# A two-layer diffusion backbone with 64 experts: the experts' down weights move from SyncE's DMA queue to ScalarE's

## What is computed

```python
scores = jax.nn.sigmoid(t @ router_w)              # 64 experts, groups of 8, the best 8 of 4 groups
gate = jnp.einsum('tk,tke->te', wts, jax.nn.one_hot(top_e, N_EXPERTS))
act = jax.nn.silu(jnp.einsum('td,edf->tef', t, w_gate)) * jnp.einsum('td,edf->tef', t, w_up)
routed = jnp.einsum('tef,efd->td', act * gate[:, :, None], w_down)
shared = (jax.nn.silu(t @ sh_gate) * (t @ sh_up)) @ sh_down
```

## Time and profile before

| | us |
|---|---|
| median of 3 runs | 1647.92 (1643.26 to 1652.52) |
| the profiled execution, its own time | 1641.82 |
| its span in the trace | 1640.2 |
| TensorE busy | 1474.5 |
| ScalarE busy | 260.6 |
| VectorE busy | 460.2 |

### The profile page before, as it was taken

The page is one execution under the profiler, slowest core; times in us unless marked ns, Lnnn a source line. Parts: engine busy times, 40 slices in busy tenths (PEclk is TensorE's granted clock), DMA queues, the critical chain, the costliest instruction groups (busy, mean ns, idle before and its releaser), DMA issues. The chain is left out here.

```text
span 1640.2 us, 28207 instructions
## 1 busy us (share of the span) xinstructions
PE 1474.5 (90%) x12120; PEld 781.4 (48%) x12121; DVE 460.2 (28%) x956; ACT 260.6 (16%) x441; POOL 107.2 (7%) x349
## 2 busy tenths in 40 slices
PE   3899988999898989899869998989999999999995
PEld 3665755634343434344346667564344334334441
DVE  1291875311110111111134548470111111111112
ACT  1223103311010111111013221051111111111110
POOL 2600520000000000000000024000000000000000
PEclk8899999899999999999979999989999999999998
DMA  6755940499999999899744778008999999999994
GB/s 244 254 186 209 327 168 1 192 388 408 387 421 388 418 387 418 361 422 405 329 172 148 273 255 305 7 38 350 407 380 418 375 413 381 418 389 385 395 422 181
DMA packets 109253, 509.56 MB, mean 311 GB/s; under 512 B 12865, under 2 KB 14653, under 8 KB 59197
## 3 DMA queue, kind: packets, MB, share of 16 engines
q1 hardware_dynamic: 108508, 506.52, 77.5%
q0 software_dynamic: 384, 1.05, 0.2%
q10 hardware_dynamic: 224, 0.06, 0.0%
HBM read 505.49 MB, written 2.10 MB: 309 GB/s over the span
## 5 line engine op out<-in xcount | busy, mean ns | idle before, releaser
L916 PE MATMUL ps<-ring,h 128*32 128x512 f32 x3328 | 389.0, 621 | 70.4 <-DMA ring<-in_exp_w_up 42.0
L916 PEld LDWEIGHTS ps<-ring,h 128*32 128x32 f32 x3328 | 117.4, 114 | 336.8 <-issue 336.7
L935 PE MATMUL ps<-ring,mid 128*32 128x512 f32 x1664 | 200.1, 598 | 3.1 <-DVE hT L1522 1.6
L942 PE MATMUL ps<-hT,mid 128*128 128x512 f32 x416 | 192.4, 605 | 1.6 <-DVE hT L1530 1.6
L902 PEld LDWEIGHTS ps<-tm,mid 128*128 128x128 bf16 x2496 | 144.4, 98 | 44.3 <-issue 43.1
L902 PE MATMUL ps<-tm,mid 128*128 128x128 bf16 x2496 | 156.9, 219 | 0.3
L1520 DVE TENSOR_TENSOR mid<-mid,ps 128x256 f32<-128x256 f32 x52 | 21.9, 422 | 460.9 <-ACT mid L1216 460.9
L942 PEld LDWEIGHTS ps<-hT,mid 128*128 128x128 f32 x416 | 74.7, 189 | 120.0 <-issue 116.5
L1522 DVE COPY hT<-ps 128x512 f32<-128x512 f32 x52 | 36.0, 692 | 328.9 <-PE ps L935 328.9
L1216 ACT ACTIVATE mid<-ps 128x256 f32<-128x256 f32 x52 | 20.0, 384 | 532.0 <-PE ps L916 532.0
L650 PE MATMUL ps<-ring,hT 128*128 128x512 f32 (+1 forms) x256 | 97.9, 541 | 0.0
(11 more groups left out here) (273 smaller groups left out, 1153.4 us busy)
## 6 DMA issues: line engine op xcount, KB each, us to landing
ring<-in_exp_w_gate SPq DMA_DIRECT2D x128, 1024.0 KB, 10.7
ring<-in_exp_w_up SPq DMA_DIRECT2D x128, 1024.0 KB, 12.9
ring<-in_exp_w_down SPq DMA_DIRECT2D x128, 1024.0 KB, 13.7
ring<-in_w_ada SPq DMA_DIRECT2D x28, 2048.0 KB, 10.0
ring<-in_w_in SPq DMA_DIRECT2D x6, 2048.0 KB, 13.1
ring<-in_w_out SPq DMA_DIRECT2D x4, 2048.0 KB, 7.9
ring<-in_w_in SPq DMA_DIRECT2D x2, 3072.0 KB, 16.7
ring<-in_w_in SPq DMA_DIRECT2D x2, 2176.0 KB, 9.7
```

The lines of the kernel that those rows point to most:

```text
L916: last = mm(ps[first:first + TILE, 4, :], X_e[:, b, kt, first:first + TILE], gate_up(ring[:, slot, :], kt), start=(kt == 0), stop=(kt == K ...
L935: last = mm(ps[first:first + TILE, 7, :], turn[:, P * j + first:P * j + first + TILE], down(ring[:, slot, :], j, half), start=(j == 0), st ...
L942: last = mm(bank(2 * st + half), turn[:, FF + P * st:FF + P * (st + 1)], Y[:, 512 * half:512 * (half + 1)], start=False, stop=False, skip_ ...
```

## The change

SyncE asks for gate and up weights alone. ScalarE asks for the down weights: those of k = 0, 1, 2 after its first copy of gathered tokens, that of k = 3 after the shared expert, and after its copies of pass p those of every k whose slot pass p has used (`load_expert_down`, after a wait for `Y_shown` of pass p). Each read of an expert's number for a down weight is added on ScalarE. `load_down`, the slots, the semaphores and the sums on TensorE are as before.

```diff
             for p in range(PASSES):
-                wave = [k for k in range(EXPERTS) if EXPERT_PASS[k] == p]
-                e = {}
-                for k in wave:
+                for k in [k for k in range(EXPERTS) if EXPERT_PASS[k] == p]:
                     r = LOADED[k][1]
-                    e[k] = sp.value_load(order_i[0:1, r:r + 1], min_val=0, max_val=EXPERTS - 1)
+                    e = sp.value_load(order_i[0:1, r:r + 1], min_val=0, max_val=EXPERTS - 1)
                     gate_up_free(k)
                     load_gate_up(sp, ring[:, expert_slot(k), :],
...
-                for k in wave:
-                    if k >= SLOTS:
-                        sp.wait_ge(s["Y_shown"], 2 * EXPERT_PASS[k - SLOTS] + 2)
-                    load_down(sp, ring[:, expert_slot(k), :], A["exp_w_down"][layer, bass.ds(e[k], 1)][0],
-                              down_in[expert_slot(k)])
...
+            def load_expert_down(k):
+
+                r = LOADED[k][1]
+                e = act.value_load(order_i[0:1, r:r + 1], min_val=0, max_val=EXPERTS - 1)
+                load_down(act, ring[:, expert_slot(k), :], A["exp_w_down"][layer, bass.ds(e, 1)][0],
+                          down_in[expert_slot(k)])
+
             act.wait_ge(s["X_shown"], 1)
             keep_X(0, 0).then_inc(s["X_kept"], 1)
+            act.wait_ge(s["order_ready"], 1)
+            act.wait_ge(s["go_ready"], STREAMS)
+            for k in range(PRE_SLOTS):
+                load_expert_down(k)
...
             act.wait_ge(s["sh_done"], STREAMS)
+            load_expert_down(PRE_SLOTS)
...
+                following_downs = [k for k in range(SLOTS, EXPERTS) if EXPERT_PASS[k - SLOTS] == p]
+                if following_downs:
+                    act.wait_ge(s["Y_shown"], 2 * p + 2)
+                for k in following_downs:
+                    load_expert_down(k)
```

More of the change, by code:

```diff
@@ L536, in _ @@
             for p in range(PASSES):
-                wave = [k for k in range(EXPERTS) if EXPERT_PASS[k] == p]
-                e = {}
-                for k in wave:
+                for k in [k for k in range(EXPERTS) if EXPERT_PASS[k] == p]:
                     r = LOADED[k][1]
-                    e[k] = sp.value_load(order_i[0:1, r:r + 1], min_val=0, max_val=EXPERTS - 1)
+                    e = sp.value_load(order_i[0:1, r:r + 1], min_val=0, max_val=EXPERTS - 1)
                     gate_up_free(k)
                     load_gate_up(sp, ring[:, expert_slot(k), :],
-                                 [A[w][layer, bass.ds(e[k], 1)][0] for w in ("exp_w_gate", "exp_w_up")],
+                                 [A[w][layer, bass.ds(e, 1)][0] for w in ("exp_w_gate", "exp_w_up")],
                                  gate_in[expert_slot(k)])
-                for k in wave:
-                    if k >= SLOTS:
-                        sp.wait_ge(s["Y_shown"], 2 * EXPERT_PASS[k - SLOTS] + 2)
-                    load_down(sp, ring[:, expert_slot(k), :], A["exp_w_down"][layer, bass.ds(e[k], 1)][0],
-                              down_in[expert_slot(k)])
         def rsqrt_dve(link, ss, v, r0, t, r, scale):
```

## The result

The changed kernel takes 1697.89 us in the median (1696.38 to 1706.3, 4 runs) against 1648.76 us (4 runs) of the kernel before. The ratio is 1.0316, interval 1.0285 to 1.0346: 3% slower, 49 us. The forecast was 1693 within 1658 to 1724. The two profiled executions lie further apart than the medians, by 57 us (1641.82 and 1699.09); the forecast of 51 more was counted from the profiled 1641.8.

A forecast was written before the change was run, and what follows sets the result against it. It took TensorE and the weights' DMA as close limits, the weights tighter, with about 4% of holes in the queue. Terms summed to 25.5 us a layer, 51 for both, on the profiled 1641.8: 1693 us, range 1658 to 1724.

The forecast's parts named there:

- Step 2: At passes 5, 9, 13, early down weights share the rate and delay gate and up: 5.1 us each, 15.3 a layer.
- Step 3: At passes 18 and 25, the same delay with other lead-ins: up to 2.9 us, taken as 1.5 each, 3.0 a layer.
- 4: pass 21: At pass 21, with three experts, a loss between nothing and 5.1 us, taken as 2.5 a layer.
- Step 5: At passes 3, 7, 11, 15, 20, second behind a pass of four, late gate and up: 0.6 us each, 3.0.
- step 6: At pass 2, gate and up finds an empty queue and comes earlier: a gain of 1.2 us a layer.
- Step 7: At the start, three reads and requests on ScalarE delay its copies, so the shared down product stands 2.9 us a layer.
- 8: requests in the passes: Behind a pass of four, four reads and requests on ScalarE take 6.0 us within a 7.05 us product: costs nothing.
- Step 1: Requests leaving SyncE let pass 7's gate and up be asked for earlier, but full DMA engines move nothing earlier: nothing.
- Faster: Rival, 8%: gate and up keeps its rate and down fills the holes alone; 1623 us, or 1604 with all holes.
- little: Rival, 6%: losses near 2 us at passes of four, given back by bandwidth and pass 2; within 8 us.
- Order of arrival: Rival, 8%: transfers served in order of request; passes 5, 9, 13 lose 2.3 us, five down products 2.7; 1686 us.
- ScalarE late: Part of the forecast's upper end, no chance of its own: requests of 2 us, 12 us more, 1705 us.

## Why the prediction was right, point by point

The time was right by its main mechanism: down bytes got ahead of the last gate and up weights of passes 5, 9 and 13. It was near to the number by sizes that made up for each other, and that part is luck. For a layer, as the mean of both:

| step of the prediction | forecast us | measured us |
|---|---|---|
| 2: passes 5, 9, 13 | 15.3 | 14.2 |
| 3: passes 18 and 25 | 3.0 | 0.2 |
| 4: pass 21 | 2.5 | 2.3 |
| 5: passes 3, 7, 11, 15, 20 | 3.0 | 0 |
| 6: pass 2 | -1.2 | -1.2 |
| 7: the start | 2.9 | 2.2 |
| 8: requests in the passes | 0 | 0 |
| not in it: wait ahead of pass 1 | - | 1.9 |
| not in it: down product behind a pass of four | - | 4.9 |
| not in it: slower gate and up products | - | 6.1 |
| not in it: passes 6, 10, 14, 19 | - | -0.4 |
| sum | 25.5 | 30.2 |

*Step 1, nothing moves earlier:* right. Gate of pass 7's first expert is asked for at 437.2, 3.3 us behind that of pass 6's, and the queue is full from there.

*Step 2, the main term:* right in sum, 9.2, 8.8, 8.0 us in layer 0 and 8.6, 8.0, 8.1 in layer 1, six waits of 50.5 us for 22.1. Its working had gate and up seen 5.1 us late, and the waits grew by 4.7 in the mean.

Two things in it were off, and they nearly cancel. The first byte of a down weight was put 1.2 us behind its request; it came 3.5 us behind it. So when the second two down weights began to move, at 419.6 and not at 416.6, only 0.38 million bytes of gate and up were left, 0.9 us at the full rate. By an estimate, equal shares would have made 1.8 us of them and let pass 5 start at about 422.5, with the prediction's own 1.1 us behind the last byte. It started at 424.45, since the last bytes went at much less than a half.

The assumption of equal shares held where both queues had much to do, 209 against 217 GB/s in one of the stretches above, and not at the end of gate and up, 74 against 336 and 45 against 381. The rule of the Trainium skill, DMA: Bandwidth & Descriptors, section Queues, rings and completion order, that a DMA engine takes turns between the queues that have work, agrees with the halves. The end would agree with it too if only some of the 16 engines still had gate and up bytes, but the trace does not tell the engines apart. That spreading requests brings no bandwidth, as the rules for kernel authors on that page of the Trainium skill say, agrees with 422 against 418 GB/s.

*Step 5, and the last section's "no wait of over 1 us ahead of L935":* this failed, and waits there were one of the prediction's own signs of being wrong. The prediction had half rate begin with the first down bytes at 439.7, 2.1 us behind the end of the pass of four, and so made gate and up of pass 7 late and left pass 6's down weights in time. But q10 started 3.5 us behind its request, at 448.6, and shared with gate and up of pass 7 from there to 460. The loss falls the other way round: pass 7 doesn't wait, and pass 6's second down weight, asked for at 446.2, takes 14.1 us and lands at 460.3, 1.6 us late. Waits of 1.2 to 2.0 us stand ahead of six of the down products, 4.9 us a layer that the sum put at nothing.

*Step 3* was mis-sized; passes 18 and 25 wait 15.8 us in all for 15.4. The queue had run far enough ahead there, which was the lower end of that step's bound; in layer 1 pass 18 lost 1.5 us and pass 25 gained 0.9.

*Step 7* was mis-sized by 0.7: a read with its request is 1.15 us on ScalarE and not 1.3. What it left out is that down of k = 3 now stands in part ahead of gate and up of k = 4, and pass 1 waits 1.9 us.

*The clock* was in step 6 alone, as a possible gain at pass 2. That gain came, 4.2 us over both layers (products of 7.07 us for 8.40 and 9.98). But passes 5, 9, 13 lost 6.5, pass 14 lost 5.6 and pass 21 lost 4.2. In all the gate and up products are 12.1 us longer, and the prediction's sum had none of that. The length of a wait doesn't settle the price: pass 19 waits 2.1 and 2.3 us and then runs in 8.77 us in one layer and in 7.07 in the other.

*Rivals.* "Faster" and "little" fall with the result. "Order of arrival" is out by the halves above; its wait ahead of the down product does appear, but beside a shared rate. Its order on one queue was tried by itself, and its forecast of 1686 is near the 1682 measured, but only its wait ahead of the down product came: ahead of passes 5 and 9 stand 3.6 and 3.5 us where it had 5.9. "ScalarE late" didn't happen: requests and reads of four take 4.6 us inside a product of 7.05.

What stays open: why a queue whose neighbour is full needs 3.5 us for its first byte where it needs 1.0 otherwise, and how the last bytes of gate and up are spread over the DMA engines. No experiment isolates either. That about one transfer of the neighbour, 2.5 us of work, is already handed to the engines and stands ahead would fit the first, and is only argued. Why pass 5 waits less, and pass 25 so much more, in the run with only wide passes on ScalarE wasn't worked out.

## What to carry to other kernels

When one in-order queue feeds an engine at nearly the rate of the DMA engines, its order is a priority: keep what the next product waits for ahead of what it needs later. A second queue takes half of the rate for whatever it carries, 3.5 us behind its request here, however urgent the first queue's transfers are, and it doubles the time of their last bytes. Before moving requests to an idle engine, ask what is ahead of the last critical transfer now, and what will be; a request with its read cost about a microsecond here, each MB in front two and a half. And an order by the moment at which slots come free isn't the order of need: it cost 36 us on a single queue.

## What was not expected of the hardware

A transfer of 1 MB on a queue that had been idle landed 4.8 us behind its request with the DMA engines free, and 9.2 us with the other queue full. Of the 9.2, 3.5 passed before its first byte. In the changed kernel's trace it is 3.4 to 3.5 us for most requests beside a full queue, and never more. It is 1.0 us for all twelve requests that found the DMA engines free in the run with the wide passes' down weights behind their gate and up.

Two queues shared evenly only in the middle: the last 0.25 million bytes of one took 3.0 to 3.6 us beside a full second queue, for 1.4 to 1.8 alone, while the second moved 1.1 to 1.4 million.

And parts of the change were not additive: 14 us for the narrow passes with the start, 81 for the wide ones, 49 for all.
